# Weight chunks of a two-layer decoder trunk: rounded and split in two halves, the vector engine's first half moved ahead of the take-over

## What is computed

```python
def _forward(x, mC, mn, mm, ssm, sconv, fconv, p):
    ...
    for i in range(DEPTH):
        hn = _rmsnorm(x, p['norm_mix'][i])
        if i % N_MIXERS == 0:
            out, C, n, m = _mlstm_mixer(hn, mC[j], mn[j], mm[j], p['a_w_in'][j], p['a_b_if'][j], p['a_w_out'][j])
        else:
            out, s_new, c_new = _mamba_mixer(hn, ssm[j], sconv[j], p['b_w_in'][j], p['b_conv_w'][j], p['b_conv_b'][j],
                                             p['b_dt_bias'][j], p['b_A_log'][j], p['b_D'][j], p['b_norm_w'][j], p['b_w_out'][j])
        x = x + out.astype(x.dtype)
        hn = _rmsnorm(x, p['norm_ffn'][i])
        out, fb = _conv_ffn(hn, fconv[i], p['f_w_up'][i], p['f_conv_w'][i], p['f_conv_b'][i], p['f_w_down'][i])
        x = x + out.astype(x.dtype)
    y = _rmsnorm(x, p['norm_final'])
```

## Time and profile before

| | |
|---|---|
| median of three runs | 3262.29 us |
| the profiled execution | 3262.68 us |
| its span, first to last instruction | 3261.1 us |
| PE busy | 3102.9 us, 95% |
| DVE busy | 2100.4 us, 64% |
| ACT busy | 1336.1 us, 41% |
| POOL busy | 865.0 us, 27% |
| mean granted clock of PE | 0.980 |

### The profile page before, as it was taken

How to read it: one execution, slowest core, us unless ns; L and a number is a source line. 1 busy time by engine, 2 the same in 40 slices (tenths; PEclk the granted TensorE clock), 3 DMA queues, 4 the chain that set the end, 5 groups by cost and what they waited for, 6 DMA issues and landing times.

```text
span 3261.1 us, 63483 instructions
## 1 busy us (share of the span) xinstructions
PE 3102.9 (95%) x23228; PEld 3035.5 (93%) x23228; DVE 2100.4 (64%) x3130; ACT 1336.1 (41%) x1741; POOL 865.0 (27%) x1139
## 2 busy tenths in 40 slices
PE   7999999999999999989888988988899999999997
PEld 7999999999999999988888888988899999999997
DVE  5555657766446775567776676677677664567744
ACT  5333335444334444443443343344344443344432
POOL 2111113323002332224442343344333220133311
PEclk8999999999999999999999999999899999999998
DMA  5454454444454444554454454554544445544444
GB/s 198 157 190 166 168 181 158 165 167 155 160 175 167 162 160 152 176 168 168 157 184 167 168 175 173 176 179 170 188 157 166 167 150 166 174 165 160 155 161 144
DMA packets 91405, 545.86 MB, mean 167 GB/s; under 512 B 11689, under 2 KB 12529, under 8 KB 43905
## 3 DMA queue, kind: packets, MB, share of 16 engines
q1 hardware_dynamic: 71872, 466.98, 42.2%
q0 software_dynamic: 19392, 76.98, 6.5%
HBM read 510.92 MB, written 32.99 MB: 167 GB/s over the span
## 4 chain that ended last, share of the span: by engine, by line
PE 77%; issue 7%; DVE 6%; POOL 4%; ACT 4%; DMA 2%; DVEq 0%; POOLq 0%; ACTq 0%; SPq 0%
PE ps L407 25%; PE ps L408 24%; PE ps L409 24%; PE ps L414 4%; DMA b_s<-b_s_in 2%; ACT w_hi L705 2%; POOL b_xw L1714 1%; DVE w_lo L1056 1%; DVE b_u L1416 1%; POOL b_s L1748 1%; POOL b_new L1696 1%; DVE work L1504 0%; DVE sumsq L1499 0%; DVE b_u L1418 0%; DVE b_u L1414 0%
## 5 line engine op out<-in xcount | busy, mean ns | idle before, releaser
L407 PE MATMUL ps<-hn_hi,w_hi 128*128 128x288 f32 x4896 | 1470.2, 300 | 31.1 <-DVE w_lo L1056 17.3
L408 PE MATMUL ps<-hn_lo,w_hi 128*128 128x288 f32 x4896 | 1455.1, 297 | 0.0
L409 PE MATMUL ps<-hn_hi,w_lo 128*128 128x288 f32 x4896 | 1450.1, 296 | 0.0
L1056 DVE TENSOR_TENSOR w_lo<-w_raw,w_hi 128x2048 fp32r<-128x2048 f32 (+1 forms) x482 | 1024.8, 2126 | 570.5 <-ACT w_hi L705 570.5
L705 ACT ACTIVATE w_hi<-w_raw 128x2048 fp32r<-128x2048 f32 (+1 forms) x482 | 857.8, 1780 | 1080.8 <-PE ps L409 1067.8
L407 PEld LDWEIGHTS ps<-hn_hi,w_hi 128*128 128x128 f32 x4896 | 929.1, 190 | 42.6 <-issue 22.7
L409 PEld LDWEIGHTS ps<-hn_hi,w_lo 128*128 128x128 f32 x4896 | 932.4, 190 | 0.0
L408 PEld LDWEIGHTS ps<-hn_lo,w_hi 128*128 128x128 f32 x4896 | 930.5, 190 | 1.0
L1659 POOL COPY f_new<-f_pad 128x2 f32 x176 | 238.4, 1354 | 1074.0 <-ACT f_u L882 1074.0
L407 PE MATMUL ps<-act_hi,w_hi 128*128 128x288 f32 x1408 | 413.8, 294 | 4.9 <-DVE w_lo L1056 4.7
L408 PE MATMUL ps<-act_lo,w_hi 128*128 128x288 f32 x1408 | 415.4, 295 | 0.0
(11 more groups left out here) (286 smaller groups left out, 3192.0 us busy)
## 6 DMA issues: line engine op xcount, KB each, us to landing
w_raw<-wf_up_in SPq DMA_DIRECT2D x176, 1024.0 KB, 4.9
w_raw<-wf_down_in SPq DMA_DIRECT2D x128, 704.0 KB, 4.0
w_raw<-wb_in_in SPq DMA_DIRECT2D x80, 1024.0 KB, 4.9
w_raw<-wa_in_in SPq DMA_DIRECT2D x48, 1024.0 KB, 5.0
w_raw<-wb_out_in SPq DMA_DIRECT2D x32, 1024.0 KB, 4.9
w_raw<-wa_out_in SPq DMA_DIRECT2D x16, 1024.0 KB, 5.0
b_sT<-b_sT_in POOLq DMA_DIRECT2D x32, 512.0 KB, 4.2
b_s<-b_s_in POOLq DMA_DIRECT2D x32, 512.0 KB, 5.1
```

Source lines behind the costliest of these rows:

```text
L407: nc.tensor.matmul(out, w_hi[:, s, col], hi[:, t, :], start=first and k == 0, stop=False)
L408: nc.tensor.matmul(out, w_hi[:, s, col], lo[:, t, :], start=False, stop=False)
L409: m = nc.tensor.matmul(out, w_lo[:, s, col], hi[:, t, :], start=False, stop=end)
L1056: TT(w_lo[:, s, 0:cols], w_raw[:, s, 0:cols], w_hi[:, s, 0:cols].bitcast(F32), ALU.subtract).then_inc(w_low, 1)
```

## The change

A chunk is worked on in two halves: the front is its first 1024 columns (8 tiles), the back is the rest (1024 columns, or 384 in a chunk of 11 tiles). ACT rounds the front when PE has finished the front of chunk c-2 (a new semaphore, `front_done`, marked by the third matmul of tile 7), and the back when PE has finished chunk c-2. DVE's remainder is two instructions, one for each half; `w_high` and `w_low` count two for each chunk. PE waits for the front at the start of a chunk and for the back ahead of tile 8. SP waits for both halves.

On DVE the front of chunk c+2 now stands directly ahead of the take-over of chunk c, in A, in B, in the up projections of F and in the chunks of the out projections; the back stands where the split stood. In the down projections of F both halves stand behind the take-over. Where the split of before made sure that a take-over had been done, PE gets a wait of its own on `res_added` (three places).

```diff
+FRONT = CH // 2
...
-                wait(sp, w_low, c.plus(-1))
+                wait(sp, w_low, c.plus(-1).times(2))
...
-                wait(pe, w_low, c.plus(1))
+                if at == 0:
+                    wait(pe, w_low, c.times(2).plus(1))
                 s, out = c.base % 2, ps[:, bank, 0:T]
                 for k, t in enumerate(tiles):
+                    if at + k == FRONT // P:
+                        wait(pe, w_low, c.times(2).plus(2))
...
+                    if at + k == FRONT // P - 1:
+                        m.then_inc(front_done, 1)
...
             def split(c, cols=CH):

                 wait(act, raw_landed[c.base % 2], c.half().plus(1).times(16))
+                wait(act, front_done, c.plus(-1))
+                A(w_hi[:, c.base % 2, 0:FRONT], w_raw[:, c.base % 2, 0:FRONT], ACT.Copy).then_inc(w_high, 1)
                 wait(act, chunk_done, c.plus(-1))
-                A(w_hi[:, c.base % 2, 0:cols], w_raw[:, c.base % 2, 0:cols], ACT.Copy).then_inc(w_high, 1)
+                A(w_hi[:, c.base % 2, FRONT:cols], w_raw[:, c.base % 2, FRONT:cols], ACT.Copy).then_inc(w_high, 1)
...
+            def low_part(c, cols):
+                s = c.base % 2
+                TT(w_lo[:, s, cols], w_raw[:, s, cols], w_hi[:, s, cols].bitcast(F32), ALU.subtract).then_inc(w_low, 1)
+
+            def front(c):
+
+                wait(dve, w_high, c.times(2).plus(1))
+                low_part(c, slice(0, FRONT))
+
+            def back(c, cols=CH):
+
+                wait(dve, w_high, c.times(2).plus(2))
+                low_part(c, slice(FRONT, cols))
+
             def split(c, cols=CH):
-
-                wait(dve, w_high, c.plus(1))
-                s = c.base % 2
-                TT(w_lo[:, s, 0:cols], w_raw[:, s, 0:cols], w_hi[:, s, 0:cols].bitcast(F32), ALU.subtract).then_inc(w_low, 1)
+                front(c)
+                back(c, cols)
...
             def out_chunk(c, n0, m, t, k=None, then=None):

+                front(c.plus(2))
                 wait(dve, chunk_done, c.plus(1))
...
-                split(c.plus(2))
+                back(c.plus(2))
...
+                    if not (mixed is None and j == 0):
+                        front(u.times(6).plus(C_AIN + j + 2))
...
                             ahead = first_pair and j == 0
+                            front(c.plus(2))
                             if ahead:
-                                norm(k, lambda: split(c.plus(2)))
+                                norm(k, lambda: back(c.plus(2)))
...
+                    front(c.plus(j + 2))
                     b_take(u, p, c, j)
                     if mixes and even:
                         b_mix(mixed, 1 - p, j + 1)
-                    split(c.plus(j + 2))
+                    back(c.plus(j + 2))
```

More of the change, by code:

```diff
@@ L267, in trunk @@
         raw_landed = [sem("raw_landed0"), sem("raw_landed1")]
-        w_high, w_low, chunk_done, proj_taken, res_added = map(sem, (
-            "w_high", "w_low", "chunk_done", "proj_taken", "res_added"))
+        w_high, w_low, front_done, chunk_done, proj_taken, res_added = map(sem, (
+            "w_high", "w_low", "front_done", "chunk_done", "proj_taken", "res_added"))
         consts_in, norm_w_in, y_ready, y_stored = map(sem, (
@@ L552, in up_four @@
                         if first and j == 0:
+                            wait(pe, res_added, ed0 - 3)
                             first_project(c, bank, k)
@@ L675, in _ @@
             with pe.Fori(0, 2) as i:
+                wait(pe, res_added, Count(ED_BIN - 3, (i, KT)))
                 for n in range(2):
@@ L679, in _ @@
                          [Count(4 + k + 1, (i, 8)) for k in range(8)])
+            wait(pe, res_added, ED_BIN + 2 * KT - 3)
             b_group(Count(6), 0, Count(C_BIN + 76), Count(5))
@@ L1265, in a_head @@
                     if not (mixed is None and j == 0):
-                        split(u.times(6).plus(C_AIN + j + 2))
+                        back(u.times(6).plus(C_AIN + j + 2))
                     if mixed is None:
```

## The result

The changed kernel takes 3228.99 us (median of four runs, 3225.58 to 3231.04), the kernel before 3261.72 us in the runs beside it; the ratio is 0.9899, with an interval of 0.9882 to 0.9916. The profiled execution took 3231.04 us, its span is 3229.5 us, and the granted clock is 0.979, as before (0.980). Its lines are L714 and L716 for ACT's two halves (L705 before), L1065 for DVE's halves (L1056), L411 to L413 for the projection's matmuls, L420 and L441 for those of the mixing, L1501 for `b_dec` (L1474), L1518 for the sums into `b_s` (L1491).

The account below looks back on a forecast made before the run. PE, busy 95% of the span, was taken as the bound, its stops as the gain. 3262.68 us, minus 11.4 outside B's groups and 3 inside, gave 3248.3, so 3248; range 3230 to 3268, its own 3241 to 3253.

Parts of the forecast that it names:

- the charge for the hoist at odd j: Mixing groups of B: front ahead of take-over makes b_dec 0.6 us later, PE waits 15 to 21 times, +9.0 to +12.6.
- at most 5.7 given back at `b_s`: Even j of B's groups: DVE through 0.27 us sooner, 21 waits for the state, 0 to -5.7 us.
- The gates: Around B's gates: three PE stops shortened, -1.1 at 1395.50, -1.5 at 1444.69 and -1.9 at 1464.01; -4.5 us forecast.
- the stop of 7.07 us: Start, at 54.05: front ahead of the take-over saves some 1.4 us; chunks before it 1.1 more; -2.5 for the start.
- The stop of 1.59 us at 1444.69: Gates of B: a half and the take-over would be saved, no more than the stop; -1.5 us.
- the one of 5.55: Gates of B, at 1464.01: chain with a 1.54 us wait for ACT and a whole remainder shortens; -1.9 us.
- The four stops of 1.1 us: F, starts of down projections, as at 823.25: DVE's chain ends 1.9 us sooner, stops gone; -4.4 us.
- rival 4: Marks or waits inside chunks cost PE under 10 ns each, +4.8 us: 3253, with lost start gains 3258; chance 0.05.
- j = 9 and j = 0: Seven groups of B: j = 9, ahead of the norm, -1.4 each, -10.1 us; j = 0 like an even one, -1.9.
- Rival 3: Groups of B: POOL's copy slips through, b_s transfer goes out 1.9 us sooner; -22, 3226, half of it 3237; chance 0.17.
- Rival 2: Groups of B: POOL's decay takes DVE's place between halves and holds the front, +20 us; slower, 3271; chance 0.14.
- Rival 1: Groups of B: time only shifts, odd j cost 12.6, waits for b_s eat half of the -12.0; 3257; chance 0.18.

Follow-up runs that it names:

- e4: Changed kernel with DVE's front put back behind take-over and decays only at odd j below 9 of the mixing groups: 3225.61 us, ratio 0.9879.
- e10: Changed kernel with DVE's front ahead of the take-over only at odd j below 9 of the mixing groups, behind it elsewhere: 3229.47 us, ratio 0.9905.
- e1: Changed kernel with DVE's front put back beside the back, behind the take-over, in all stages; halves kept on all engines: 3225.98 us, ratio 0.9883.
- e5: Changed kernel with DVE's front behind every take-over, and POOL's b_s load at j = 1, 3, 5 ahead of its b_xw products: 3217.89 us, ratio 0.9863.
- e9: Changed kernel, DVE's front behind the take-over at odd j below 9 of mixing groups, and POOL's b_s load ahead of its b_xw products: 3216.57 us, 0.9857.
- e7: Kernel before, with only DVE's remainder cut into two instructions back to back, one mark at the end: 3260.84 us, ratio 0.9997.
- e3: Changed kernel with seven extra 128x128 copies on POOL ahead of the b_new copy of j = 3 and 5: 3253.9 us, ratio 0.9969.

## Why the prediction was off

The sign was right. The size was not: of the 17 us between forecast and result, 9 lie in the groups of B, 4 at the gates, 3 in F, 1 at the start, as the table shows. The step that failed is the charge for the hoist at odd j, that PE waits for the later `b_dec` and the groups pay +9.0 to +12.6 us for it, with at most 5.7 given back at `b_s`. So the two waits were to grow by 3.3 to 12.6 us in sum; they fell by 5.8, from 64.2 to 58.4. e4 and e10 price the hoist at odd j at 3 to 7 us. The rest are terms that were too small or missing.

**The gates: half of the term was left out.** At 1395.50 I credited PE with one half of DVE, -1.1. ACT's half stood in the same chain, so the stop fell from 3.88 us to 1.46, by 2.4; both halves together, 1.06 and 1.13, make 2.2 of it.

Timeline of PE in the kernel after, the four stops (before: the earlier trace rows).

```profile
50.54 0.58 PE L411 MATMUL ps<-hn_hi,w_hi 128*128 128x288 f32 x1 [6.38 <-DVE w_lo L1065]
...
1384.70 0.37 PE L411 MATMUL ps<-hn_hi,w_hi 128*128 128x288 f32 x1 [1.46 <-DVE w_lo L1065]
...
1429.74 0.37 PE L411 MATMUL ps<-hn_hi,w_hi 128*128 128x288 f32 x1
...
1447.86 1.22 PE L420 MATMUL ps<-b_xdt,mean_mat 64*128 64x512 f32 x1 [4.34 <-DVE b_xdt L1416]
```

At the start the stop of 7.07 us lost 0.7 where 1.4 were forecast, but PE came to it 2.8 us sooner (44.16 after, 46.98 before), where 1.1 were taken, of 0 to 2.2. The stop of 1.59 us at 1444.69 is gone, as forecast; the one of 5.55 lost 1.2, not 1.9. And a second thing came with the shorter stop. The 48 matmuls that follow it, in the kernel before and after:

```profile
1395.50:1404.50 9.00, 9.00 (x48) 9.00 (x49) 7.32 (x11) 4.64 (x5) 2.55 (x3) 0.68 0.58 187
```

```profile
1384.70:1391.20 6.50, 6.50 (x49) 6.50 (x50) 5.95 (x8) 2.94 (x4) 0.00 (x0) 1.00 0.61 202
```

Behind the stop of 3.88 us the granted clock was 0.68 over the stretch, which is part of it at the lower level, 1.2 GHz; behind the stop of 1.46 us it was 1.00, all of it at 2.4 GHz. That gave 2.5 us more in the chunk behind the stop. I had no such term.

**F.** The four stops of 1.1 us went, as said, and gave 1.3 each. Short waits of 0.2 to 0.5 us, most of them at the starts of projections, went too; I had counted only stops of over 1 us. The window of F in the kernel after (before: the earlier trace rows):

```profile
1010.00:1110.00 100.00, 100.00 (x752) 100.00 (x751) 71.59 (x133) 48.87 (x71) 12.29 (x45) 1.00 0.49 168
```

Still one matmul each 133 ns. So the marks and waits inside a chunk cost PE nothing that a row shows, and rival 4 does not hold. The 26.3 ns of the Trainium skill ("TensorE: Matmul & The Clock Gate", section "The cost: per-tile semaphore tail"), which that page fits to small tiles packed in the array, are not seen here, at one mark in 24 matmuls: by them the 100 us would hold an estimated three matmuls fewer; they hold one fewer, the step of the count.

**The groups: each single price was about right, the sum was not.** The changed kernel's DVE at j = 9 of the group ahead of that of the earlier trace rows, take-over to product:

```profile
1633.97 0.46 DVE L1432 TENSOR_TENSOR b_io<-ps,rstd 128x288 f32<-128x288 f32 x1 [0.88 <-PE ps L413]
1635.07 1.23 DVE L1065 TENSOR_TENSOR w_lo<-w_raw,w_hi 128x1024 fp32r<-128x1024 f32 x1 [0.63 <-ACT w_hi L716]
1636.21 0.45 DVE L1452 SCALAR_TENSOR_TENSOR b_io<-work,b_io 128x288 f32<-128x288 f32 x1
```

The product begins 2.24 us behind the take-over's start; before it was 4.15: -1.9 where -1.4 was forecast. In each of the seven groups it is so within 0.1 us. In e1 it is 2.64, so 1.5 of the 1.9 come without the hoist: what went is above all the 1.49 us of standing for ACT. The norm and j = 0 follow on DVE, and the gain comes out at PE's stop for `b_xdt` behind them. That stop in the kernel before, and the same place after:

```profile
1674.89 0.28 PE L435 MATMUL ps<-ident,b_io 128*32 128x128 f32 x1 [2.37 <-DVE b_xdt L1444]
```

```profile
1649.94 0.61 PE L441 MATMUL ps<-ident,b_io 128*32 128x128 f32 x4
```

From the starts of the chunks, the stretch from j = 1 to j = 2 became 10.5 us shorter in sum over seven groups; -10.1 and -1.9 were forecast for j = 9 and j = 0. That size stands, in part by luck: e1 has 9.5 us of it, and the forecast had worked it out from the order.

Odd j, the price of the hoist: rows of the changed kernel at j = 3, DVE and POOL (before: the earlier trace rows).

```profile
1676.90 1.23 DVE L1065 TENSOR_TENSOR w_lo<-w_raw,w_hi 128x1024 fp32r<-128x1024 f32 x1 [0.43 <-ACT w_hi L714]
1678.04 0.42 DVE L1429 TENSOR_TENSOR b_pad<-ps,rstd 128x256 f32<-128x256 f32 x1
...
1681.22 1.02 DVE L1501 TENSOR_TENSOR b_dec<-b_dec,b_cb 128x832 f32<-128x832 f32 x1
...
1679.55 0.19 POOL L1724 COPY b_new<-b_pad 128x3 f32<-128x3 f32 x1 [3.79 <-ACT b_u L958]
...
1679.81 1.55 POOL L1713 COPY b_pad<-b_old 128x24 f32<-128x24 f32 x1
...
1682.45 0.54 POOL L1772 DMA_DIRECT2D b_s<-b_s_in  x1
```

DVE was ready at 1676.47, 0.43 ahead of the front, and `b_dec` was ended 5.77 us later; before it was 5.26 (1701.66 to 1706.92), in e1 5.32. So the step "b_dec comes 0.6 us later" held, with 0.5. What failed is the next one, "PE waits for it, 15 to 21 times, +9.0 to +12.6". PE's waits for `b_dec` did grow by 12.2 us, but those for `b_s`, which follow them in the next chunk, shrank by 18.0. The hoist alone is seen between e1 and e10: `b_dec` from 35.3 to 45.2 us, `b_s` from 21.1 to 14.7. The state comes at POOL's pace; a PE that is later at `b_dec` waits less for `b_s`. Added up, the two are 64.2 us before, 58.4 after, 56.4 in e1, 59.9 in e10.

PE's waits in e1_old_place, then in e10_odd_only:

```profile
PE ps L420 <- DVE b_dec L1497: 35.3, 18, 5.1
PE ps L420 <- DVE b_s L1514: 21.1, 14, 2.7
```

```profile
PE ps L420 <- DVE b_dec L1497: 45.2, 20, 5.1
...
PE ps L420 <- DVE b_s L1514: 14.7, 16, 1.6
```

I had charged the one in full and priced the other by DVE's chain alone, as if each reached the end.

**Rival 3 came nearest to the time, by a wrong reason.** The copy of j = 3 shows 0.19 us, as it said. But the fill behind it took 1.55 us, and the load went out 5.98 us after DVE was ready, against 6.60 before (1708.26 - 1701.66): 0.6 sooner, not 1.9. At j = 5, with no fill, it went out 1.6 us sooner (1702.35 - 1696.29 against 1728.68 - 1720.98). So a part of the rival's reason came, but e1, whose copies are held for 3.70 us and whose load is no sooner (6.67), is no slower. What the lateness of the load costs is shown by e5 beside e1 and by e9 beside e4, where it is taken away: 6.5 to 9 us, by ratios or by times.

POOL's load of `b_s` at j = 3 and j = 5 of the kernel before, then at j = 5 after:

```profile
1708.26 0.54 POOL L1744 DMA_DIRECT2D b_s<-b_s_in  x1
...
1728.68 0.54 POOL L1744 DMA_DIRECT2D b_s<-b_s_in  x1
```

```profile
1702.35 0.53 POOL L1772 DMA_DIRECT2D b_s<-b_s_in  x1
```

**Rival 2** came only at the edge. No front was held by POOL's decay. Three of the backs in the seven groups were, where the decay had begun ahead of them; one of them, on DVE and POOL:

```profile
1977.56 1.93 DVE L1065 TENSOR_TENSOR w_lo<-w_raw,w_hi 128x1024 fp32r<-128x1024 f32 x1 [0.63 <-ACT w_hi L716]
...
1976.51 1.89 POOL L1776 TENSOR_TENSOR b_s<-b_s,b_fade 128x1024 f32<-128x1024 f32 x1 [4.51 <-DMA b_s<-b_s_in]
```

The three took 1.75 to 1.95 us in place of 1.2, about 2 us more in sum, not 20. At even j DVE's time from the take-over to the end of the remainder went from 3.56 us to 3.12 with its wait for the front (1666.10 to 1669.22), and to 2.78 in e1.

**Rival 1** named the bound that came next, the transfer of `b_s`, and was wrong on the size.

**What I had missed as a whole.** The prediction priced the edit as one of order, the hoist, and the cut as its small cost, 0.06 us a pair. The cut was the gain. The rows had 570 us of DVE's standing for ACT (377.8 + 192.8), and I used them only at single stops and at j = 2 and j = 9, and put what they gave down to the order.

## What to carry to other kernels

When one engine waits for a whole instruction of another and a third waits for the second, cut the instruction on both sides of the hand-over; a cut of the second engine alone gave nothing here. Look first at where the second engine stands idle, and only then at moving work in its order: a wait that is moved ahead of other work is a wait that nothing fills. Do not take the sum of that standing for the gain; 39 us came of 447 here. Two waits in a row on one engine that hang on different chains are one budget: much of what the first takes longer the second takes shorter (9.9 and 6.4 us between e1 and e10), so price their sum.

## What the runs showed of the hardware

Two halves back to back held POOL nearly as one whole did. The copy of three columns that began 0.07 us behind DVE's first half in e1 lasted 3.70 us, past both halves and past the product for `b_dec`; between instructions of DVE that read PSUM it took 0.19 us, in the changed kernel. The mean of the 48 copies says the same for the kernel before, e7, e1 and after.

```profile
L1696 POOL COPY b_new<-b_pad 128x3 f32<-128x3 f32 x48 | 79.4, 1654 | 268.6 <-ACT b_u L947 268.6
```

```profile
L1698 POOL COPY b_new<-b_pad 128x3 f32<-128x3 f32 x48 | 67.5, 1406 | 270.7 <-ACT b_u L947 270.7
```

```profile
L1719 POOL COPY b_new<-b_pad 128x3 f32<-128x3 f32 x48 | 74.7, 1556 | 261.8 <-ACT b_u L958 261.8
```

```profile
L1724 POOL COPY b_new<-b_pad 128x3 f32<-128x3 f32 x48 | 14.5, 303 | 294.0 <-ACT b_u L958 294.0
```

The Trainium skill, "SBUF — State Buffer", section "Who interferes with whom", has the exclusion between such a pair of instructions; that the end of one DVE instruction does not let the other engine in when the next one follows at once is what these rows add.

A stop of PE can be paid twice. In e3 the groups became 23.7 us longer than in the changed kernel (679.10 and 655.40): 14.6 us of that is PE standing, and 9.1 us is PE being busy longer with the same matmuls. The granted clock over the seven windows was 0.93 in the mean in e3 and 0.95 in the changed kernel.
